# Grouped attention's product with the values: from eight f32 matmuls a group to eight fp32r matmuls on split operands

## The chip, the cores and the metric

The kernel runs on one core of one Trainium2 chip. The metric is device microseconds for one execution. The engines that matter here are TensorE (PE, with its weight loads as PEld), VectorE (DVE), ScalarE (ACT), GpSimd (POOL) and SyncE (SP), which issues the DMAs of the weights. The engines run side by side and are tied together by semaphores only.

## What is computed

A trunk of two layers over 256 tokens of width 2048: attention in two head groups, a recurrent block, cross-attention into 256 memory tokens and a gated feed-forward block per layer, all in f32. The change touches the second head group of the first layer: 16 query heads of 64, which share 2 key and value heads (8 queries each), in chunks of 64 tokens; every chunk sees itself and the one before it. Its core in the reference is:

```python
s = jnp.einsum('bcqkgd,bcjkd->bkgcqj', qc, kb).astype(jnp.float32) * (Dh ** -0.5)
s = jnp.where(valid[None, None, None, :, None, :], s, -1e30)
...
p = jax.nn.softmax(jnp.concatenate([s, sink], axis=-1), axis=-1)[..., :-1].astype(v.dtype)
o = jnp.einsum('bkgcqj,bcjkd->bcqkgd', p, vb)
```

The last line is the product with the values. Heads of one group share `vb`.

## The kernel before

**Weights.** All weights come as one stream of units (128 x 1024 values) through four slots. For each unit ACT rounds the f32 values to fp32r (`w_hi`, line 309) and DVE subtracts that from the values (`w_lo`, line 315). A product of such split operands is made of three fp32r matmuls: high by high, high by low, low by high. ACT's split of a unit waits until PE has used the unit four before it, since the slot must be free.

**Attention.** Its 32 heads go through in eight groups of four heads, `g` = 0 to 7. Groups 0 to 3 are the first head group, 4 to 7 the second. Each has these steps:
- PE: `scores(g)` into PSUM banks 0 to 2.
- DVE: `softmax(g)`: mask or bias, row maxima (line 1406 and on), which free the banks. ACT: `exps(g)`, the exponentials with row sums. DVE: `normalise(g)` (line 1431).
- PE: `turn(g)`, twelve transposes of 128x128 (line 632) into banks 3 to 5. The first 128 queries see one block of 128 keys, the last 128 two, so every head has three blocks.
- ACT copies banks 3 and 4 to `probsT` (line 1000), DVE bank 5 (line 1420).
- PE: `values(g)`, eight matmuls in f32 (line 647) into banks 4 and 5. Even heads of the group go to one bank and odd heads to the other. For groups 4 to 7 the stationary operand is `bv2`, which holds the 64 value columns twice, so that the result of a head stands in the upper and in the lower 64 partitions, of which one half is kept.
- DVE: `outputs(g)`, two copies of 64x512 to `oT` (line 1438). After the last group ACT and DVE split `oT` into `a_hi` (line 1031) and `a_lo` (line 1444) for the output projection, whose matmuls are lines 342 and 346.

**The order.** Every engine runs its own list, written out by hand. Between the attention steps PE has 32 weight units of the memory's key and value projection (lines 382 and 387), which keep it busy while the other engines work. For group `g` PE's list is: scores of `g+1`, one unit, `turn(g)`, one unit, `values(g)`, then two units (one in groups 5 and 6, none in 7). DVE's list is: softmax of `g+1`, its part of the transposed copy of `g`, splits of two units, outputs of `g`, normalising of `g+1`, splits of the units that are left. ACT's list is: the split of a unit, its part of the transposed copy of `g`, exponentials of `g+1`, the splits of the other units. In groups 1 and 5 DVE also makes the mean squares of the memory's keys (line 1297), GpSimd raises them to the power -1/2 (line 1792), and DVE scales the keys (line 1382); in group 6 PE transposes them. In group 7 DVE makes the first two low parts of `oT` before `outputs(7)`.

The first lines of `turn` and `values` hold the waits that matter: `turn(g)` waits for `normalise(g)`, for ACT's copy of group `g-1` and for `outputs(g-1)`. `values(g)` waits for both copies of group `g`.

Of the kernel before, what the change touches and what calls it, by code (L numbers as in the profile page):

```python
# [16 lines left out]
P = 128  # L17
D_MODEL, SEQ, N_MEM = 2048, 256, 256
KT = D_MODEL // P
TT = SEQ // P  # L20
# [12 lines left out]
COLS = 512  # L33
# [48 lines left out]
def trunk(nc, t):  # L82
# [3 lines left out]
    with ctx:  # L86
# [80 lines left out]
        assert O0 + 16384 + 1536 + 2048 <= FFN  # L167
        probs = at("probs", XG, [2, 3 * COLS])
        probsT = at("probsT", XG + 12288, [3 * COLS])
        bv2 = at("bv2", XG + 24576, [TT, B_KV_HEADS, 2, HEAD_DIM])  # L170
        bias_at = [at("bias0", FFN + size([4, SEQ + 2]) + size([4, SEQ]), [3 * COLS]), at("bias1", XG + 12288 + 6144, [3 * COLS])]
        mem_sq = [at("mem_sq0", FFN + 4096, [TT, XA_W]), vmem[1]]

# [49 lines left out]
        exp_done, prob_ready, bv2_ready = sem("exp_done"), sem("prob_ready"), sem("bv2_ready")  # L223
        pT_ps, pT_act, pT_dve, o_ps, o_done = sem("pT_ps"), sem("pT_act"), sem("pT_dve"), sem("o_ps"), sem("o_done")
        oT_hi, oT_lo = sem("oT_hi"), sem("oT_lo")

        proj_free = sem("proj_free")

# [297 lines left out]
        def block_done(name, b0, pos):  # L526
# [3 lines left out]
                return q if u == UNITS[name] - 1 else None  # L530
            return pos // UNITS[name] if pos % UNITS[name] == UNITS[name] - 1 else None

        def head_of(j):

            return 2 * (j % 2) + j // 2
# [3 lines left out]
        def _(pe):  # L539
# [80 lines left out]
            def turn(g):  # L620
                pb = probs[:, g % 2, :]

                pe.wait_ge(prob_ready, g + 1)
                if g:

                    pe.wait_ge(pT_act, g)
                    pe.wait_ge(o_done, g)

                for o in range(4):
                    for e, src in enumerate((8 + o, 2 * o, 2 * o + 1)):  # L630
                        n = 3 * o + e
                        last = nc.tensor.transpose(ps[:, 3 + n // 4, (n % 4) * P:(n % 4 + 1) * P], pb[:, src * P:(src + 1) * P],  # L632
                                                   ident[:, :])
                last.then_inc(pT_ps, 1)

            def values(g):

                pe.wait_ge(pT_act, g + 1)
                pe.wait_ge(pT_dve, g + 1)
                if g == 4:  # L640
                    pe.wait_ge(bv2_ready, 1)
                for j in range(4):
                    o, pair = 3 * head_of(j) * P, 2 * g + j // 2

                    for kt in range(TT):
                        val = v[:, kt, pair * P:(pair + 1) * P] if g < 4 else bv2[:, kt, (g - 4) // 2, :, :].rearrange("p e d -> p (e d)")
                        last = nc.tensor.matmul(ps[:, 4 + j % 2, (j // 2) * SEQ + kt * P:(j // 2 + 1) * SEQ], val,  # L647
                                                probsT[:, o + 2 * kt * P:o + (2 + kt) * P],
                                                start=kt == 0, stop=kt == 1, skip_group_check=True)
                last.then_inc(o_ps, 1)  # L650

            def turn_keys(l, g):
# [14 lines left out]
            for g in range(8):  # L667
                after_scores, after_turn, after_values = BETWEEN[g]
                if g < 7:
                    scores(g + 1)  # L670
                for f in after_scores:
                    mem_unit(f)
                turn(g)
                for f in after_turn:
                    mem_unit(f)
                values(g)
                for f in after_values:
                    if f == after_values[-1] and g in KEYS_TURNED:
                        turn_keys(KEYS_TURNED[g], g)
                    mem_unit(f)  # L680
# [188 lines left out]
        def _(act):  # L869
# [125 lines left out]
            def transposed(g):  # L995
# [3 lines left out]
                    act.wait_ge(o_ps, g)  # L999
                A(probsT[:, 0:2 * COLS], flat(ps[:, 3:5, :]), ACT.Copy).then_inc(pT_act, 1)  # L1000

            ch.link(act, A(lam[:, 0, :], rconst[:, :, 7], ACT.Abs))
            A(lam[:, 1, :], lam[:, 0, :], ACT.Exp, scale=-1.0).then_inc(sp_exp, 1)
# [5 lines left out]
            for g in range(8):  # L1010
                after_scores, after_turn, after_values = BETWEEN[g]
                if g in MEM_EVAC:
                    mem_evac(MEM_EVAC[g])
                for f in after_scores:
                    split_next(f)
                transposed(g)
                if g < 7:
                    exps(g + 1)
                for f in after_turn:
                    split_next(f)  # L1020
                for f in after_values:
                    if f == after_values[-1] and g in KEYS_TURNED:
                        keys_turned(KEYS_TURNED[g])
                    split_next(f)
# [242 lines left out]
        def _(dve):  # L1267
# [117 lines left out]
            def softmax(g):  # L1385
                pb, nm = probs[:, g % 2, :], neg_max[:, g % 2, :]
                dve.wait_ge(s_ps, g + 1)
                if g >= 2:

                    dve.wait_ge(pT_ps, g - 1)  # L1390
                s = HEAD_DIM ** -0.5
                if g < 4:
                    dve.wait_ge(bias_ok, g + 1)
                    last = V.scalar_tensor_tensor(pb, flat(ps[:, 0:3, :]), s, bias_at[g % 2][:, :], ALU.mult, ALU.add)
                else:
                    V.scalar_tensor_tensor(pb[:, 0:2 * COLS].rearrange("p (h n) -> p h n", h=4),
                                           flat(ps[:, 0:2, :]).rearrange("p (h n) -> p h n", h=4), s,
                                           mask[:, 0:SEQ].unsqueeze(1).to_broadcast([P, 4, SEQ]), ALU.mult, ALU.add)
                    last = V.scalar_tensor_tensor(pb[:, 2 * COLS:].rearrange("p (h n) -> p h n", h=4),
                                                  ps[:, 2, :].rearrange("p (h n) -> p h n", h=4), s,  # L1400
                                                  mask[:, SEQ:SEQ + P].unsqueeze(1).to_broadcast([P, 4, P]), ALU.mult, ALU.add)
                last.then_inc(s_used, 1)
                dve.wait_ge(s_used, g + 1)
                if g >= 2:
                    dve.wait_ge(exp_done, g - 1)
                V.tensor_reduce(nm[:, 0:4], pb[:, 0:2 * COLS].rearrange("p (h n) -> p h n", h=4), op=ALU.max, axis=X)
                ch.link(dve, V.tensor_reduce(nm[:, 4:8], pb[:, 2 * COLS:].rearrange("p (h n) -> p h n", h=4), op=ALU.max, axis=X))
                if g < 4:
                    V.tensor_scalar(nm, nm, -1.0, None, ALU.mult).then_inc(nmax_ready, 1)
                else:  # L1410
                    ch.link(dve, V.tensor_tensor(nm, nm, sinks[:, g - 4, :], ALU.max))
                    ch.link(dve, V.tensor_scalar(nm, nm, -1.0, None, ALU.mult))
                    V.tensor_tensor(sink_e[:, g % 2, :], sinks[:, g - 4, :], nm, ALU.add).then_inc(nmax_ready, 1)

            def transposed(g):
# [3 lines left out]
                    dve.wait_ge(o_ps, g)  # L1419
                V.tensor_copy(probsT[:, 2 * COLS:3 * COLS], ps[:, 5, :]).then_inc(pT_dve, 1)  # L1420

            def normalise(g):

                dve.wait_ge(exp_done, g + 1)
                sm, pb = sums[:, g % 2, :], probs[:, g % 2, :]
                if g >= 4:
                    ch.link(dve, V.tensor_tensor(sm, sm, sink_e[:, g % 2, :], ALU.add))
                ch.link(dve, V.reciprocal(rsum[:, :], sm))
                for cols, heads, keys in ((slice(0, 2 * COLS), slice(0, 4), SEQ), (slice(2 * COLS, 3 * COLS), slice(4, 8), P)):
                    x = pb[:, cols].rearrange("p (h n) -> p h n", h=4)  # L1430
                    last = V.tensor_tensor(x, x, rsum[:, heads].unsqueeze(2).to_broadcast([P, 4, keys]), ALU.mult)
                last.then_inc(prob_ready, 1)

            def outputs(g):
# [3 lines left out]
                    last = V.tensor_copy(flat(oT[part, 2 * g:2 * g + 2, :]), ps[part, 4 + e, :])  # L1438
                last.then_inc(o_done, 1)

            def low_outputs(b):

                dve.wait_ge(oT_hi, b + 1)
                V.tensor_tensor(pair_tiles(a_lo, 2 * b, 2), oT[:, 2 * b:2 * b + 2, :], pair_tiles(a_hi, 2 * b, 2).bitcast(F),  # L1444
                                ALU.subtract).then_inc(oT_lo, 1)
# [7 lines left out]
            for g in range(8):  # L1453
                after_scores, after_turn, after_values = BETWEEN[g]
                if g < 7:
                    softmax(g + 1)
                transposed(g)
                for f in after_scores:
                    split_next(f)
                if MEM_EVAC.get(g) in (0, 2):  # L1460
# [4 lines left out]
                    keys_normed(MEM_EVAC[g] // 2)  # L1465
                if g == 7:

                    dve.wait_ge(pT_act, 8)
                    dve.wait_ge(yT_done, len(NORMED) + 2)
                    for _ in range(2):  # L1470
                        V.engine_nop().then_inc(proj_free, 1)
                    for b in range(2):
                        low_outputs(b)
                outputs(g)
                if g < 7:
                    normalise(g + 1)
                for f in after_values:
# [1 line left out]
                if g == 0:  # L1479

                    dve.wait_ge(tok_free, TOK.index("bkv") + 1)
                    for e in range(2):
                        last = V.tensor_copy(bv2[:, :, :, e, :], bv[:, :, :].rearrange("p t (h d) -> p t h d", h=2))
                    last.then_inc(bv2_ready, 1)
            for b in range(2, 8):
                low_outputs(b)

# [516 lines left out]
```

## Time and profile before

| | us |
|---|---|
| median of 3 runs | 2323.28 (2323.11 to 2323.39) |
| profiled execution | 2323.38 |
| its span on the core | 2321.7 |
| PE busy in the span | 2299.5 (99%) |
| DVE busy | 1580.0 (68%) |
| ACT busy | 1243.2 (54%) |
| granted clock of PE, mean | 1.00 |

The profile shows one execution. A line of a view names the kernel line, the engine, the operation and the tiles (result <- operands) with partitions x elements. A time in brackets at the end of a row is idle time of that engine just before it, and who ended it. Matmuls overlap, so the time from one start to the next says more than the duration of one.

### The profile page before, as it was taken

To read this page: it belongs to the slowest core of one execution; us is meant where nothing else is said; L and a number is where in the kernel's file an instruction comes from. 1 tells how busy PE (TensorE), PEld (TensorE's weight loads), DVE (VectorE), ACT (ScalarE), POOL (GpSimd) and SP (SyncE) were. 2 spreads that over 40 slices of the span, in tenths; PEclk is the share of its full clock that TensorE was granted. 3 is DMA by queue.
4 is the path that set the end of the run, shared out by engine and by line. 5 is a ranking of instruction groups with operands and counts; after the bars stand their busy time and mean duration, and the time that the engine had idled before them with its cause. 6 is when DMAs were issued, how large, how long until landed. Compare 5 with 4: busy or idle time off the path is not lost.

```text
span 2321.7 us, 38274 instructions
## 1 busy us (share of the span) xinstructions
PE 2299.5 (99%) x13164; PEld 2002.4 (86%) x13164; DVE 1580.0 (68%) x1958; ACT 1243.2 (54%) x1701; POOL 205.8 (9%) x188
## 2 busy tenths in 40 slices
PE   8999999999999999999999999999999999999999
PEld 6888888988888888888888888898888888888888
DVE  7766776577777777755556778667777777774443
ACT  5655555465555555544444776555555555553332
POOL 5620001230000000000000100222000000000000
PEclk9999999999999999999999999999999999999999
DMA  7556435544555555565555555545555555556554
GB/s 269 201 195 199 132 121 178 172 154 164 198 187 184 183 189 197 190 196 189 190 190 184 180 189 178 199 134 177 176 196 191 191 181 183 197 190 199 187 187 160
DMA packets 118941, 426.93 MB, mean 184 GB/s; under 512 B 13600, under 2 KB 14496, under 8 KB 118864
## 3 DMA queue, kind: packets, MB, share of 16 engines
q1 hardware_dynamic: 117072, 418.36, 54.0%
q0 software_dynamic: 1792, 7.52, 1.0%
q8 instruction: 51, 0.84, 0.2%
q14 instruction: 26, 0.21, 0.0%
HBM read 423.73 MB, written 2.10 MB: 183 GB/s over the span
## 4 chain that ended last, share of the span: by engine, by line
PE 95%; DVE 3%; ACT 1%; issue 1%; DMA 0%; SPq 0%; ACTq 0%; DVEq 0%
PE ps L342 51%; PE ps L346 25%; PE ps L382 7%; PE ps L387 4%; PE ps L327 2%; PE ps L363 2%; DVE w_lo L315 1%; PE ps L647 1%; PE ps L834 1%; ACT w_hi L309 0%; PE ps L632 0%; DVE xg_hl L1273 0%; PE ps L717 0%; DMA xT<-in_x_t 0%; PE ps L556 0%
## 5 line engine op out<-in xcount | busy, mean ns | idle before, releaser
L315 DVE TENSOR_TENSOR w_lo<-raw,w_hi 128x1024 fp32r<-128x1024 f32 x788 | 961.6, 1241 | 497.4 <-ACT w_hi L309 493.0
L309 ACT ACTIVATE w_hi<-raw 128x1024 fp32r<-128x1024 f32 x787 | 812.3, 1056 | 558.6 <-PE ps L346 420.5
L342 PE MATMUL ps<-xg_hl,w_hi 128*128 128x512 f32 x3328 | 1047.0, 396 | 5.9 <-DVE w_lo L315 5.9
L346 PEld LDWEIGHTS ps<-xg_hl,w_lo 128*128 128x128 f32 x3328 | 625.2, 188 | 147.8
L346 PE MATMUL ps<-xg_hl,w_lo 128*128 128x256 f32 x3328 | 653.8, 278 | 0.0
L342 PE MATMUL ps<-a_hl,w_hi 128*128 128x512 f32 x1920 | 603.0, 395 | 0.6 <-DVE a_hl L1444 0.6
L342 PEld LDWEIGHTS ps<-xg_hl,w_hi 128*128 128x128 f32 x3328 | 506.9, 189 | 7.3 <-DVE w_lo L315 7.1
L346 PEld LDWEIGHTS ps<-a_hl,w_lo 128*128 128x128 f32 x1920 | 360.7, 188 | 85.3
L346 PE MATMUL ps<-a_hl,w_lo 128*128 128x256 f32 x1920 | 377.1, 278 | 0.0
L342 PEld LDWEIGHTS ps<-a_hl,w_hi 128*128 128x128 f32 x1920 | 292.2, 189 | 0.7 <-DVE w_lo L315 0.7
L1154 ACT ACTIVATE y_buf<-u_buf,fconv 128x256 f32<-128x256 f32 x176 | 96.7, 597 | 231.1 <-DVE u_buf L1619 231.1
L382 PE MATMUL ps<-w_hi,xg_hl 128*128 128x512 f32 (+1 forms) x576 | 137.9, 383 | 7.4 <-DVE xg_hl L1273 6.4
L1626 DVE SCALAR_TENSOR_TENSOR y_buf<-u_buf,fconv,y_buf 128x256 f32<-128x256 f32 x176 | 85.2, 485 | 82.4 <-ACT y_buf L1154 81.7
L382 PEld LDWEIGHTS ps<-w_hi,xg_hl 128*128 128x128 f32 x576 | 104.1, 190 | 28.1 <-issue 6.9
L1149 ACT ACTIVATE a_hl<-y_buf 128x512 f32 (+1 forms) x44 | 27.9, 633 | 103.9 <-DVE y_buf L1648 103.9
L1662 DVE TENSOR_TENSOR u_buf<-cross,ps 128x512 f32<-128x512 f32 x84 | 57.8, 688 | 34.4 <-ACT cross L1188 34.3
L1631 DVE SCALAR_TENSOR_TENSOR y_buf<-u_buf,fconv,y_buf 128x256 f32<-128x256 f32 x176 | 77.1, 480 | 0.1
L387 PE MATMUL ps<-w_lo,xg_hl 128*128 128x512 f32 (+1 forms) x288 | 73.9, 381 | 1.2 <-DVE w_lo L315 1.1
L382 PE MATMUL ps<-w_hi,a_hl 128*128 128x512 f32 x256 | 66.1, 400 | 0.9 <-ACT kmem_tok L967 0.6
L387 PEld LDWEIGHTS ps<-w_lo,xg_hl 128*128 128x128 f32 x288 | 52.1, 189 | 13.0 <-DVE w_lo L315 3.2
L1140 ACT ACTIVATE y_buf<-y_buf 128x512 f32<-128x512 f32 x44 | 27.9, 634 | 61.2 <-DVE y_buf L1631 61.1
L1273 DVE SCALAR_TENSOR_TENSOR xg_hl<-xT,gains,xg_hl 128x256 fp32r<-128x256 f32 (+1 forms) x96 | 55.2, 601 | 7.7 <-ACT xg_hl L874 7.5
(197 smaller groups left out, 1533.7 us busy)
## 6 DMA issues: line engine op xcount, KB each, us to landing
raw<-in_w_stream SPq DMA_DIRECT2D x787, 512.0 KB, 4.1
bias<-in_rel_bias POOLq DMA_DIRECT2D x4, 768.0 KB, 6.3
memT<-in_mem_t POOLq DMA_DIRECT2D x4, 512.0 KB, 6.6
gate_w<-in_gate_w POOLq DMA_DIRECT2D x4, 512.0 KB, 3.9
out_t<-xT SPq DMA_DIRECT2D x8, 256.0 KB, 4.1
xT<-in_x_t SPq DMA_DIRECT2D x2, 512.0 KB, 8.6
xT<-in_x_t SPq DMA_DIRECT2D x3, 256.0 KB, 7.7
raw<-in_w_stream SPq DMA_DIRECT2D x2, 256.0 KB, 3.2
```

Of the source, the lines that this page charges most:

```text
L309: nc.scalar.activation(w_hi[:, s, :], raw[:, s, :], ACT.Copy).then_inc(hi_done, 1)
L315: nc.vector.tensor_tensor(w_lo[:, s, :], raw[:, s, :], w_hi[:, s, :].bitcast(F), ALU.subtract).then_inc(lo_done, 1)
L327: last = nc.tensor.matmul(ps[:, bank, 0:SEQ], a[:, s, w], b[:, k0 + k, :], start=start and k == 0 and q == 0, stop=stop and k == nk - 1 an ...
L342: nc.tensor.matmul(ps[:, bank + m, :], w_hi[:, s, w], both, start=start and k == ks[0], stop=False, skip_group_check=True)
L346: last = nc.tensor.matmul(ps[:, bank + m, SEQ:2 * SEQ], w_lo[:, s, w], x[:, xk, 0, :], start=False, stop=stop and k == ks[-1], skip_group_ ...
L382: nc.tensor.matmul(ps[:, bank + tt, 0:n], a[:, k0 + k, tt * P:tt * P + P], w_hi[:, s, k * n:k * n + n], start=start and k == 0 and q == 0, ...
L387: last = nc.tensor.matmul(ps[:, bank + tt, 0:n], hi[:, k0 + k, tt * P:tt * P + P], w_lo[:, s, k * n:k * n + n], start=False, stop=stop and ...
L1154: A(y_buf[:, m, :], u_buf[:, m, 2:2 + SEQ], ACT.Identity, scale=column(fconv, w + 2, i, 32), bias=column(fconv, w + 3, i, 32)).then_inc(ta ...
L1273: V.scalar_tensor_tensor(dst, src, gain, hi.bitcast(F), ALU.mult, ALU.subtract).then_inc(count, 1)
L1626: middle.append(ch.mark(V.scalar_tensor_tensor(y_buf[:, m, :], u_buf[:, m, 1:1 + SEQ], column(fconv, 4 * (4 * half + m) + 1, i, 32), y_buf ...
L1631: ins = V.scalar_tensor_tensor(y_buf[:, m, :], u_buf[:, m, 0:SEQ], column(fconv, 4 * (4 * half + m), i, 32), y_buf[:, m, :], ALU.mult, ALU ...
L1662: V.tensor_tensor(u_buf[:, tile:tile + 2, 2:2 + SEQ], cross[:, :, :], ps[:, bank:bank + 2, 0:SEQ], ALU.add).then_inc(proj_free, 1)
```

## The change

The product of groups 4 to 7 is made of fp32r matmuls on split operands. `bv_hlh` takes the place of `bv2` and holds high, low, high of the 64 value columns. Its columns 0 to 127 (high, low) are the stationary operand for the even heads of a group, columns 64 to 191 (low, high) that for the odd ones. So one matmul gives the product with the high values in the half that belongs to the head, and the product with the low values in the other. The transposed probabilities are split too: ACT rounds them to `pT_hi`, in three copies of one bank each, and DVE subtracts to `pT_lo`, in three instructions. Two heads with the same half go through one matmul: 512 columns for the first block of keys, 256 for the second, once with `pT_hi` and once with `pT_lo`. Then ACT copies the two halves with the low product to `o_low`, across the partitions, and DVE's `outputs` becomes an addition. The product of low by low is included. Groups 0 to 3 are as before.

```diff
-        bv2 = at("bv2", XG + 24576, [TT, B_KV_HEADS, 2, HEAD_DIM])
+        pT_hi = at("pT_hi", XG + 12288, [3 * COLS], R)
+        pT_lo = at("pT_lo", XG + 12288 + 6144, [3 * COLS], R)
+        bv_hlh = at("bv_hlh", XG + 24576, [TT, B_KV_HEADS, 3, HEAD_DIM], R)
+        o_low = at("o_low", XG + 24576 + 3072, [COLS])
...
+        def turned(g):
+
+            return g + 2 * max(0, g - 4)
+
...
-                last.then_inc(pT_ps, 1)
+                        if n == 11 or (g >= 4 and n % 4 == 3):
+                            last.then_inc(pT_ps, 1)
...
+            def grouped_values(g):
+
+
+                pe.wait_ge(pT_act, turned(g + 1))
+                pe.wait_ge(pT_dve, turned(g + 1))
+                if g == 4:
+                    pe.wait_ge(bv2_ready, 1)
+                hi4, lo4 = (z[:, :].rearrange("p (o b n) -> p o b n", o=4, b=3) for z in (pT_hi, pT_lo))
+                for e in range(2):
+                    out = ps[:, 4 + e, :].rearrange("p (o n) -> p o n", o=2)
+                    for kt in range(TT):
+                        val = bv_hlh[:, kt, (g - 4) // 2, e:e + 2, :].rearrange("p e d -> p (e d)")
+                        for x, part in enumerate((hi4, lo4)):
+                            p = part[:, 2 * e:2 * e + 2, 2, :] if kt else part[:, 2 * e:2 * e + 2, 0:2, :].rearrange("p o b n -> p o (b n)")
+                            last = nc.tensor.matmul(out[:, :, kt * P:SEQ], val, p, start=kt == 0 and x == 0, stop=kt == 1 and x == 1,
+                                                    skip_group_check=True)
                 last.then_inc(o_ps, 1)
...
+            def transposed_hi(g):
+                act.wait_ge(o_ps, g)
+                for x in range(3):
+                    act.wait_ge(pT_ps, turned(g) + x + 1)
+                    A(pT_hi[:, x * COLS:(x + 1) * COLS], ps[:, 3 + x, :], ACT.Copy).then_inc(pT_act, 1)
+
+            def low_halves(g):
+
+                act.wait_ge(o_ps, g + 1)
+                if g > 4:
+                    act.wait_ge(o_done, g)
+                A(o_low[0:64, :], ps[64:P, 4, :], ACT.Copy)
+                A(o_low[64:P, :], ps[0:64, 5, :], ACT.Copy).then_inc(o_low_ready, 1)
+
...
                 for f in after_turn:
                     split_next(f)
+                if g >= 4:
+                    low_halves(g)
...
+            def transposed_lo(g):
+                dve.wait_ge(o_ps, g)
+                for x in range(3):
+                    dve.wait_ge(pT_act, turned(g) + x + 1)
+                    cols = slice(x * COLS, (x + 1) * COLS)
+                    V.tensor_tensor(pT_lo[:, cols], ps[:, 3 + x, :], pT_hi[:, cols].bitcast(F), ALU.subtract).then_inc(pT_dve, 1)
+
...
+            def grouped_outputs(g):
+                dve.wait_ge(o_low_ready, g - 3)
+                for e in range(2):
+                    part = slice(64 * e, 64 * e + 64)
+                    last = V.tensor_tensor(flat(oT[part, 2 * g:2 * g + 2, :]), ps[part, 4 + e, :], o_low[part, :], ALU.add)
                 last.then_inc(o_done, 1)
...
-                    for e in range(2):
-                        last = V.tensor_copy(bv2[:, :, :, e, :], bv[:, :, :].rearrange("p t (h d) -> p t h d", h=2))
-                    last.then_inc(bv2_ready, 1)
+                    whole = bv[:, :, :].rearrange("p t (h d) -> p t h d", h=2)
+                    for x in (0, 2):
+                        V.tensor_copy(bv_hlh[:, :, :, x, :], whole).then_inc(bv_hi, 1)
+                    dve.wait_ge(bv_hi, 2)
+                    V.tensor_tensor(bv_hlh[:, :, :, 1, :], whole, bv_hlh[:, :, :, 0, :].bitcast(F), ALU.subtract).then_inc(bv2_ready, 1)
```

What stands in a row on PE, at the product of group 4, before. The names are result <- operands:

```order
L387 MATMUL ps<-w_lo,a_hl 128x512 x3
L647 MATMUL ps<-probsT,bv_101 128x256 [waits bv2_ready,pT_dve,pT_act]
L647 MATMUL ps<-probsT,bv_101 128x128
L647 MATMUL ps<-probsT,bv_101 128x256
L647 MATMUL ps<-probsT,bv_101 128x128
L647 MATMUL ps<-probsT,bv_101 128x256
L647 MATMUL ps<-probsT,bv_101 128x128
L647 MATMUL ps<-probsT,bv_101 128x256
L647 MATMUL ps<-probsT,bv_101 128x128
L382 MATMUL ps<-w_hi,a_hl 128x512 [waits hi_done]
```

And the same place after:

```order
L391 MATMUL ps<-w_lo,a_hl 128x512 x3
L674 MATMUL ps<-pT_hi,bv_hlh 128x512 [waits bv2_ready,pT_dve,pT_act]
L674 MATMUL ps<-pT_lo,bv_hlh 128x512
L674 MATMUL ps<-pT_hi,bv_hlh 128x2x128
L674 MATMUL ps<-pT_lo,bv_hlh 128x2x128
L674 MATMUL ps<-pT_hi,bv_hlh 128x512
L674 MATMUL ps<-pT_lo,bv_hlh 128x512
L674 MATMUL ps<-pT_hi,bv_hlh 128x2x128
L674 MATMUL ps<-pT_lo,bv_hlh 128x2x128
L386 MATMUL ps<-w_hi,a_hl 128x512 [waits hi_done]
```

The product stays at its place between the same weight units, with as many instructions, each of them wider.

DVE in group 6, from the end of the softmax of group 7, before:

```order
L1413 TENSOR_TENSOR sink_e<-sinks,neg_max 128x8 [waits dve_self]
L1420 COPY probsT<-ps 128x512 [waits o_ps,pT_ps]
L315 TENSOR_TENSOR w_lo<-raw,w_hi 128x1024 [waits hi_done] x2
L1438 COPY oT<-ps 64x512 [waits o_ps]
L1438 COPY oT<-ps 64x512
```

DVE there after:

```order
L1461 TENSOR_TENSOR sink_e<-sinks,neg_max 128x8 [waits dve_self]
L1475 TENSOR_TENSOR pT_lo<-ps,pT_hi 128x512 [waits pT_act,o_ps]
L1475 TENSOR_TENSOR pT_lo<-ps,pT_hi 128x512 [waits pT_act] x2
L319 TENSOR_TENSOR w_lo<-raw,w_hi 128x1024 [waits hi_done] x2
L1500 TENSOR_TENSOR oT<-ps,o_low 64x512 [waits o_low_ready]
L1500 TENSOR_TENSOR oT<-ps,o_low 64x512
```

One copy became three subtractions that wait for ACT's parts, and the outputs wait for ACT's `o_low` in place of PE.

ACT in group 7, from its part of the transposed copy to the first high parts of `oT`, before:

```order
L1000 ACTIVATE probsT<-ps 128x1024 [waits o_ps,pT_ps]
L309 ACTIVATE w_hi<-raw 128x1024 [waits pe_unit,raw_full3]
L1031 ACTIVATE a_hl<-oT 128x2x256 [waits o_done,pe_unit]
L1031 ACTIVATE a_hl<-oT 128x2x256 [waits o_done]
L967 ACTIVATE vmem_60<-ps,r_tok 128x512 [waits rtok_ready,pe_unit]
```

ACT there after:

```order
L1035 ACTIVATE pT_hi<-ps 128x512 [waits pT_ps,o_ps]
L1035 ACTIVATE pT_hi<-ps 128x512 [waits pT_ps] x2
L313 ACTIVATE w_hi<-raw 128x1024 [waits pe_unit,raw_full3]
L1042 ACTIVATE o_low<-ps 64x512 [waits o_done,o_ps]
L1043 ACTIVATE o_low<-ps 64x512
L1079 ACTIVATE a_hl<-oT 128x2x256 [waits o_done,pe_unit]
L1079 ACTIVATE a_hl<-oT 128x2x256 [waits o_done]
L996 ACTIVATE vmem_60<-ps,r_tok 128x512 [waits rtok_ready,pe_unit]
```

The two copies to `o_low`, which wait for the product of group 7 (`o_ps`), stand ahead of the first high part of `oT`.

## Rows read from the trace of the kernel before

**Rows 1.** The page: busy time of each engine, and the chain that ended last.

```profile
PE 2299.5 (99%) x13164; PEld 2002.4 (86%) x13164; DVE 1580.0 (68%) x1958; ACT 1243.2 (54%) x1701; POOL 205.8 (9%) x188
...
PE 95%; DVE 3%; ACT 1%; issue 1%; DMA 0%; SPq 0%; ACTq 0%; DVEq 0%
```

**Rows 2.** Waits of PE, 290 to 348 us: us in total, times, longest.

```profile
PE ps L647 <- DVE probsT L1420: 0.8, 1, 0.8
PE ps L342 <- DVE a_hl L1444: 0.6, 1, 0.6
PE ps L382 <- ACT kmem_tok L967: 0.3, 1, 0.3
```

**Rows 3.** Groups by line and shape: busy us, mean ns of one, idle before.

```profile
L1188 ACT ACTIVATE cross<-ps 128x512 f32<-128x512 f32 x104 | 60.0, 577 | 0.0
...
L1503 DVE TENSOR_TENSOR xT<-xT,ps 128x512 f32<-128x512 f32 x16 | 11.0, 687 | 14.0 <-PE ps L346 14.0
...
L647 PE MATMUL ps<-probsT,bv 128*128 128x256 f32 x32 | 9.6, 382 | 0.8 <-DVE probsT L1420 0.8
...
L647 PE MATMUL ps<-probsT,bv 128*128 128x128 f32 x32 | 6.2, 274 | 0.0
```

**Rows 4.** Timeline of PE, then DVE, in group 4: start, duration.

```profile
297.81 2.78 PE L647 MATMUL ps<-probsT,bv 128*128 128x256 f32 x16
300.35 2.07 PE L382 MATMUL ps<-w_hi,a_hl 128*128 128x512 f32 x8
...
295.55 0.68 DVE L1420 COPY probsT<-ps 128x512 f32<-128x512 f32 x1
```

**Rows 5.** Timeline of PE in the output projection.

```profile
347.97 0.63 PE L342 MATMUL ps<-a_hl,w_hi 128*128 128x512 f32 x2
348.43 0.40 PE L346 MATMUL ps<-a_hl,w_lo 128*128 128x256 f32 x2
348.67 0.62 PE L342 MATMUL ps<-a_hl,w_hi 128*128 128x512 f32 x2
```

**Rows 6.** Timeline of DVE in group 1.

```profile
247.92 1.23 DVE L315 TENSOR_TENSOR w_lo<-raw,w_hi 128x1024 fp32r<-128x1024 f32 x1 [2.36 <-ACT w_hi L309]
```

**Rows 7.** Timelines of PE, DVE and POOL in group 5.

```profile
315.37 2.78 PE L647 MATMUL ps<-probsT,bv 128*128 128x256 f32 x16
...
312.80 0.69 DVE L1420 COPY probsT<-ps 128x512 f32<-128x512 f32 x1
...
319.71 1.22 DVE L1382 TENSOR_TENSOR kmem_tok<-kmem_tok,rq 128x1024 f32<-128x1024 f32 x1
320.85 1.39 DVE L1438 COPY oT<-ps 64x512 f32<-64x512 f32 x2
...
316.04 1.66 POOL L1792 TENSOR_TENSOR rq<-ss,neg_half 128x8 f32<-128x8 f32 x1 [63.69 <-DVE ss L1299]
```

**Rows 8.** Timelines of PE and DVE, groups 6 and 7.

```profile
330.72 2.86 PE L647 MATMUL ps<-probsT,bv 128*128 128x256 f32 x16 [0.76 <-DVE probsT L1420]
...
339.76 1.50 PE L632 MATMUL ps<-ident,probs 128*128 128x128 f32 x12
...
329.89 0.69 DVE L1420 COPY probsT<-ps 128x512 f32<-128x512 f32 x1
...
336.00 1.38 DVE L1438 COPY oT<-ps 64x512 f32<-64x512 f32 x2
```

**Rows 9.** Timelines of PE, ACT and DVE, end of group 7.

```profile
343.85 2.78 PE L647 MATMUL ps<-probsT,bv 128*128 128x256 f32 x16
347.19 0.70 PE L342 MATMUL ps<-a_hl,w_hi 128*128 128x512 f32 x2 [0.56 <-DVE a_hl L1444]
...
344.11 1.06 ACT L309 ACTIVATE w_hi<-raw 128x1024 fp32r<-128x1024 f32 x1 [1.78 <-PE ps L387]
345.07 1.14 ACT L1031 ACTIVATE a_hl<-oT 128x512 fp32r<-128x512 f32 x2
...
346.36 1.30 DVE L1444 TENSOR_TENSOR a_hl<-oT,a_hl 128x512 fp32r<-128x512 f32 x2
```

More of the change, by code:

```diff
@@ L225, in trunk @@
         oT_hi, oT_lo = sem("oT_hi"), sem("oT_lo")
+        bv_hi, o_low_ready = sem("bv_hi"), sem("o_low_ready")
         proj_free = sem("proj_free")
@@ L624, in turn @@
                 if g:
-                    pe.wait_ge(pT_act, g)
+                    pe.wait_ge(pT_act, turned(g))
+                    pe.wait_ge(pT_dve, turned(g))
                     pe.wait_ge(o_done, g)
@@ L633, in turn @@
                                                    ident[:, :])
-                last.then_inc(pT_ps, 1)
+                        if n == 11 or (g >= 4 and n % 4 == 3):
+                            last.then_inc(pT_ps, 1)
             def values(g):
[L638 to L641, printed above, removed]
+                pe.wait_ge(pT_act, turned(g + 1))
+                pe.wait_ge(pT_dve, turned(g + 1))
                 for j in range(4):
@@ L645, in values @@
                     for kt in range(TT):
-                        val = v[:, kt, pair * P:(pair + 1) * P] if g < 4 else bv2[:, kt, (g - 4) // 2, :, :].rearrange("p e d -> p (e d)")
+                        val = v[:, kt, pair * P:(pair + 1) * P]
                         last = nc.tensor.matmul(ps[:, 4 + j % 2, (j // 2) * SEQ + kt * P:(j // 2 + 1) * SEQ], val,
@@ L649, in values @@
                                                 start=kt == 0, stop=kt == 1, skip_group_check=True)
+                last.then_inc(o_ps, 1)
+            def grouped_values(g):
+                pe.wait_ge(pT_act, turned(g + 1))
+                pe.wait_ge(pT_dve, turned(g + 1))
+                if g == 4:
[9 more added lines that the diff above has]
+                                                    skip_group_check=True)
                 last.then_inc(o_ps, 1)
@@ L675, in _ @@
                     mem_unit(f)
-                values(g)
+                if g < 4:
+                    values(g)
+                else:
+                    grouped_values(g)
                 for f in after_values:
@@ L1015, in _ @@
                     split_next(f)
-                transposed(g)
+                if g < 4:
+                    transposed(g)
+                else:
+                    transposed_hi(g)
                 if g < 7:
@@ L1388, in softmax @@
                 if g >= 2:
-                    dve.wait_ge(pT_ps, g - 1)
+                    dve.wait_ge(pT_ps, turned(g - 1))
                 s = HEAD_DIM ** -0.5
@@ L1439, in outputs @@
                 last.then_inc(o_done, 1)
+            def grouped_outputs(g):
[3 more added lines that the diff above has]
+                    last = V.tensor_tensor(flat(oT[part, 2 * g:2 * g + 2, :]), ps[part, 4 + e, :], o_low[part, :], ALU.add)
+                last.then_inc(o_done, 1)
             def low_outputs(b):
@@ L1456, in _ @@
                     softmax(g + 1)
-                transposed(g)
+                if g < 4:
+                    transposed(g)
+                else:
+                    transposed_lo(g)
                 for f in after_scores:
@@ L1466, in _ @@
                 if g == 7:
-                    dve.wait_ge(pT_act, 8)
+                    dve.wait_ge(pT_act, turned(8))
                     dve.wait_ge(yT_done, len(NORMED) + 2)
@@ L1473, in _ @@
                         low_outputs(b)
-                outputs(g)
+                if g < 4:
+                    outputs(g)
+                else:
+                    grouped_outputs(g)
                 if g < 7:
```

## The prediction

> **What bounds the kernel now.** The page comes first. TensorE (PE) is busy 99% of the span, and the chain that ended last lies on it for 95% [rows 1]. So a microsecond taken from PE's stream is a microsecond of the kernel, as long as nothing else is late where it is taken. The next question is where PE is not the bound. I looked at the stretch that the change touches, groups 4 to 7 of the attention, 290 to 348 us. The waits of PE there are three and add up to 1.7 us [rows 2]: one on VectorE (DVE) for the transposed probabilities, one on DVE for the first tile of the next section, and a small one on ScalarE (ACT). The first two touch what the change makes longer. So the stretch must be walked through group by group, with the time of each engine; PE's busy share alone would mislead.
>
> **The product itself.** One group's eight f32 matmuls (each in two passes, so 16 records; the four groups have 32 of each width [rows 3]) stream 1,536 columns, and take 2.54 us from the first start to the start of the next weight unit, 297.81 to 300.35 [rows 4]. The new product has eight fp32r matmuls as well, four of 512 and four of 256 columns: 3,072 columns. Their price is not in this trace for two-part moving data, but the fp32r matmuls of the output projection have the same widths: two of 512 and two of 256 columns per step, and a step is 0.70 us, 347.97 to 348.67 [rows 5]. Twice that is 1.40 us. The bounds are 1.40 and, if the piecewise moving data took away all gain, the old 2.54; I take 1.40, since the runs of 128 or 256 neighbouring values differ little from the 512 of those rows. **Saved: 1.14 us a group, 4.6 us in all.** That is also the most that the change can give, and it is just under 0.2% of 2323.
>
> The Trainium skill, page "TensorE: Matmul & The Clock Gate", section "Back-to-back issue gap", gives about 131 ns for a matmul of 512 columns in a stream of weight loads and matmuls, and 81 ns for 128. By that, with some 100 ns for 256 columns, the product would be an estimated 0.9 us and the saving 1.6 us a group. The same rule would make the step of the output projection 0.46 us, where the trace has 0.70 [rows 5], so it is not taken here; it would change the result below by about -0.5 us.
>
> **What is added elsewhere.** (a) ACT: the copy of the transposed probabilities becomes three of 128x512 instead of one of 128x1024. Such a copy out of PSUM is 0.58 us [rows 3], so three are some 1.6 with overlap. They may begin after four of twelve transposes. (b) DVE: the one copy of 0.69 us becomes three subtractions of a PSUM and an SBUF operand, 0.69 us each by the residual addition of that shape [rows 3], 2.05 together (bounds 1.9 to 2.1). **DVE's part comes 1.4 us later than now, each time.** It stands after the softmax of the next group on DVE's queue, as before. (c) ACT: two copies of 64x512 that bring the low product to the other half, about 1.1 us, and DVE's output additions now wait for them; the additions themselves cost what the copies did. (d) DVE once, after group 0: a subtraction more, and one wait on itself, about +0.5 us; DVE sits idle for 2.36 us soon after, before the weight unit at 247.92 [rows 6], and PE does not wait there, so it costs nothing. No DMA and nothing on SyncE or GpSimd is added.
>
> **Group by group**, as PE's shift against the trace (minus is earlier).
> Group 4: the product starts at 297.81. DVE's old copy starts at 295.55 [rows 4]; the first high part is there by about then, so the three subtractions end near 297.65. No wait, by 0.1 to 0.2 us. After the product PE is at -1.1. ACT's exponentials begin some 0.3 us later, and with the low halves behind them the outputs of group 4 come about 0.3 later on DVE. I take this as absorbed before the softmax of group 6; if not, add 0.3.
> Group 5: the old copy starts at 312.80 [rows 7], held up by the softmax ahead of it, so the subtractions end at 314.9. PE, 1.1 early, is at the product at 314.3 instead of 315.37: it now waits 0.6 and starts at -0.4, and leaves at **-1.55**. On DVE the sum of squares of the memory keys comes 1.4 later, GpSimd's power of 1.66 us [rows 7] ends at 319.1 instead of 317.7, and the scaling of the keys starts there, still 0.55 ahead of the old 319.71, which waited for a weight unit. The weight unit is early because the exponentials are. So the outputs at 320.85 and everything behind them on DVE move by -0.55.
> Group 6: this is where DVE is the bound. The old copy starts at 329.89 and PE waits 0.76 for it [rows 8]. Now the start is 329.35, and three subtractions end at 331.4. PE, which comes at 328.3, waits 3.2 us and starts at 331.5 instead of 330.72. Here the whole gain so far is given back: **+0.75** at the start, -0.4 after the product. ACT's low halves then lie beside DVE's weight unit, so the outputs (now 336.00) are at -0.5, and the transposes of group 7, which waited for DVE at 339.76 [rows 8], are at -0.5.
> Group 7: no softmax is ahead, so the subtractions end under the weight unit. The product starts at 343.35 instead of 343.85, and ends at 344.75.
> The next section: its first matmul at 347.19 waits for the low part of the first tile on DVE, 346.36 to about 347.05 [rows 9]. That chain now runs from the end of the last weight unit (about 343.9) over ACT's split at 344.11 and DVE's. The change puts the low halves of group 7 on ACT ahead of the first high part (345.07), and they wait for the end of the product: 344.75, +0.25 for the signal, +1.1 for two copies, +0.55 for the high part, +0.7 for the low one, +0.05: 347.4. So the new chain is 4.0 us long from the end of that unit where the old was 3.3. **PE starts there at +0.2**, although it was done 1.6 us earlier. The later tiles follow: DVE's output additions and the third pair's low part end near 350.0, and PE, 2.8 us into the section, asks for it at 350.2. From here on the rest is PE's stream, shifted by +0.2.
>
> In gaps: 4 x -1.14 saved, +0.65 waiting in group 5, +2.3 in group 6, +1.8 before the next section, together +0.2. The profiled execution took 2323.38 with a span of 2321.7, and its time is 0.1 from the median 2323.28. **Forecast: 2323.5 us**, that is, no change.
>
> **Rivals.**
> 1. The gain stays. If DVE and ACT kept up in groups 5 and 6, PE would reach the end of the last weight unit at 3 x -1.14 = -3.4, and the new chain of 4.0 instead of 3.3 us would give +0.75 back: 2320.6. For it: three of four products start without DVE's delay today [rows 2]. Against it: group 6 already waits, and its delay grows by construction. 0.10, spread from 2320.5 to 2322.3.
> 2. The change doesn't do what it says: the new product takes as long as the old (2.54), since the moving data come in pieces. Then group 6 starts at +1.3 and keeps that, and the last chain adds 1.14 + 0.75: +3.2, 2326.5. 0.12, with the cases in between, in which ACT's or DVE's new instructions are dearer than their rows.
> 3. Slower: fp32r falls back to the f32 rate on these operands. A column then costs 2.54/1,536 us [rows 4], 3,072 of them 5.1 us, 2.5 more than now in each of four groups, with the last chain's 0.75 and group 6's 1.3: about +12, 2335. It decides for slower from some 3.4 us a group on. Against it: the fp32r steps of the projections run at 0.70 us for 1,536 columns [rows 5]. 0.04.
> 4. The forecast, with the terms' bounds (0.3 in group 4, 0.2 on each set of subtractions, some 0.1 on each signal): 2322.3 to 2324.8. 0.72. Something else that I don't see has 0.02.
>
> The likeliest case and what lies near it give the range: **2321.9 to 2325.7**. A measurement of this kernel tells a change from none at about 0.2%, 4.6 us. Faster by more would need more than the whole saving: 0.02. Slower by more is rival 3 and a rest: 0.05. Within: 0.93.
>
> **What the profile after would show.** The product: eight fp32r matmuls in 1.4 us from the first start to the next unit (2.5: rival 2, 5: rival 3). PE's waits on DVE's low part: none in group 4, 0.6 us in group 5, about 3 in group 6; if group 6 waits under 1.5, rival 1 is near. Before the output projection a gap of 2.6 us, ended by DVE's first low part, with ACT's two 64x512 copies just ahead of the first high part. Everything after 350 us at a constant shift of a few tenths. The forecast is wrong if that shift is not constant, or if the power on GpSimd, which now sets the outputs of group 5, comes later than 319.1.

## The result, and the profile after

The changed kernel takes 2326.35 us (median of 22 runs, 2323.43 to 2327.66), the kernel before 2323.09 in the same sessions (22 runs, 2322.26 to 2324.3). The ratio is 1.0012, with a 95% interval of 1.0007 to 1.0018: slower by 0.12%, about 3 us. That is less than the 0.2% that the forecast called a change, and 0.65 us above the upper end of its range of 2321.9 to 2325.7. The profiled execution took 2326.14 us with a span of 2324.3, against 2323.38 and 2321.7.

The page and the waits of PE between 290 and 350 us, which answer to [rows 1, 2]. The waits read: us in total, times, longest:

```profile
PE 2297.8 (99%) x13132; PEld 2000.1 (86%) x13132; DVE 1584.8 (68%) x1967; ACT 1247.9 (54%) x1717; POOL 206.8 (9%) x188
```

```profile
PE ps L674 <- DVE pT_lo L1475: 3.3, 2, 2.9
PE ps L346 <- DVE a_hl L1506: 2.8, 1, 2.8
PE ps L386 <- ACT kmem_tok L996: 0.3, 1, 0.3
```

PE is busy 1.7 us less in the whole span, and waits 4.7 us more in these rows. The waits on DVE are where the forecast had them: before the products of groups 5 and 6, and before the output projection.

The timeline of PE at the products of groups 4 to 7 and at the output projection, to be read against [rows 4, 7 to 9]; columns are start, duration, and in brackets the idle time before and who ended it:

```profile
297.62 0.39 PE L674 MATMUL ps<-pT_hi,bv_hlh 128*128 128x512 f32 x1
...
299.01 2.00 PE L386 MATMUL ps<-w_hi,a_hl 128*128 128x512 f32 x8
...
314.51 0.47 PE L674 MATMUL ps<-pT_hi,bv_hlh 128*128 128x512 f32 x1 [0.41 <-DVE pT_lo L1475]
...
315.97 2.00 PE L386 MATMUL ps<-w_hi,a_hl 128*128 128x512 f32 x8
...
330.82 0.62 PE L674 MATMUL ps<-pT_hi,bv_hlh 128*128 128x512 f32 x1 [2.86 <-DVE pT_lo L1475]
331.24 0.63 PE L674 MATMUL ps<-pT_lo,bv_hlh 128*128 128x512 f32 x1
...
333.38 1.54 PE L685 MATMUL ps<-ident,kmem_tok 128*128 128x128 f32 x8
334.67 2.09 PE L386 MATMUL ps<-w_hi,a_hl 128*128 128x512 f32 x8
...
340.25 1.47 PE L641 MATMUL ps<-ident,probs 128*128 128x128 f32 x12
...
344.33 0.39 PE L674 MATMUL ps<-pT_hi,bv_hlh 128*128 128x512 f32 x1
...
348.64 1.19 PE L346 MATMUL ps<-a_hl,w_hi 128*128 128x512 f32 x2 [2.76 <-DVE a_hl L1506]
...
350.06 1.05 PE L346 MATMUL ps<-a_hl,w_hi 128*128 128x512 f32 x2
...
351.34 0.69 PE L346 MATMUL ps<-a_hl,w_hi 128*128 128x512 f32 x2
```

In groups 4 and 5 the product takes 1.39 and 1.46 us. In group 6 the same eight matmuls take 2.56, from 330.82 to 333.38, and those of 512 columns follow each other by 0.42 us instead of 0.23. The first two steps of the output projection take 1.42 and 1.28 us, where a step takes 0.70 [rows 5]. Why, the view of stretches tells. Its columns are the stretch, its length, PE's busy time (matmuls), the granted clock, the DMA share and GB/s:

```profile
320.00:330.80 10.80, 7.96 (x45) 1.00 0.27 93
330.80:334.60 3.80, 3.77 (x15) 0.55 0.43 134
334.60:345.70 11.10, 11.10 (x59) 1.00 0.31 97
345.70:348.60 2.90, 0.18 (x2) 0.91 0.67 212
348.60:351.30 2.70, 2.66 (x8) 0.50 0.49 161
351.30:356.00 4.70, 4.70 (x28) 0.98 0.00 0
```

After each of the two waits of 2.8 us the granted clock is at its lower level, 0.50 or 1.2 GHz. The mean of 0.55 over the first 3.80 us says that some 3.4 us of them run at that level. At the second place it is at least the 2.7 us up to the third step, and the 0.91 of the row before says that the clock fell some 0.5 us ahead of the first matmul. From there on almost nothing more is lost: the third step begins at 351.34, 2.67 us later than in [rows 5], and the span is 2.6 us longer.

The kernel before has one wait of 0.8 and one of 0.6 us there and keeps the clock at 1.00. Its same stretches:

```profile
330.80:334.60 3.80, 3.80 (x26) 1.00 0.42 136
345.70:348.60 2.90, 2.34 (x15) 1.00 0.43 138
```

### The profile page after: what moved, and what is told of

Its sections match the earlier page's. It is cut to its first block, busy times and chain, and to the rows that moved or that the text cites. A ratio compares the mean times of both kernels' runs of the same rounds, so it can differ in the third digit from the quotient of the medians.

```text
span 2324.3 us, 38245 instructions
## 1 busy us (share of the span) xinstructions
PE 2297.8 (99%) x13132; PEld 2000.1 (86%) x13132; DVE 1584.8 (68%) x1967; ACT 1247.9 (54%) x1717; POOL 206.8 (9%) x188
## 4 chain that ended last, share of the span: by engine, by line
PE 95%; DVE 3%; ACT 1%; issue 1%; DMA 0%; SPq 0%; ACTq 0%; DVEq 0%
PE ps L346 51%; PE ps L350 25%; PE ps L386 7%; PE ps L391 4%; PE ps L331 2%; PE ps L367 2%; DVE w_lo L319 1%; PE ps L863 1%; ACT w_hi L313 0%; PE ps L655 0%; DVE xg_hl L1321 0%; PE ps L641 0%; PE ps L746 0%; DMA xT<-in_x_t 0%; PE ps L564 0%
```

## The experiments

Two theories stood at the start. A: the loss against the forecast is the clock, which falls because of the new waits. B: the matmuls after the waits are slow for a reason of their own, the operands in pieces or the other engines at work beside them.

**fill_both.** PE gets work that nobody needs in the two waits.

```diff
+            def filler(n):
+                pe.wait_ge(s_used, 8)
+                for _ in range(n):
+                    nc.tensor.matmul(ps[:, 2, 0:P], ident[:, :], ident[:, :], start=True, stop=True)
...
                 else:
+                    if g == 6:
+                        filler(12)
                     grouped_values(g)
...
                         turn_keys(KEYS_TURNED[g], g)
                     mem_unit(f)
+            filler(12)
```

> The changed kernel with PE kept busy in its two long waits: twelve f32 matmuls of identity by identity (128 columns each, into a PSUM bank that is free) before the product of group 6, and twelve before the output projection. They add nothing to the path, since PE only waits there. Theory A (the loss against the prediction is the clock, granted at half after each of the two waits of 2.8 us): the granted clock stays at 1.0, the product of group 6 takes 1.40 us again instead of 2.56, and the time falls by the lost part, some 2.5 to 3 us, to 2323.3 to 2323.9. Theory B (the matmuls after a long wait are slow for a reason of their own, such as the three-part operands or DVE and ACT working beside them): they stay at 2.56 us, and the time stays at 2326.3 or rises.

Measured: 2323.62 us (11 runs, 2322.82 to 2324.83), ratio to the kernel before 1.0001 (0.9992 to 1.0010). The stretches of this kernel, columns as above:

```profile
330.80:334.60 3.80, 3.63 (x23) 1.00 0.38 112
334.60:345.70 11.10, 11.10 (x63) 1.00 0.37 114
345.70:348.60 2.90, 2.82 (x21) 1.00 0.88 305
348.60:351.30 2.70, 2.70 (x17) 1.00 0.06 23
```

And its timeline of PE at the two places:

```profile
331.08 0.47 PE L674 MATMUL ps<-pT_hi,bv_hlh 128*128 128x512 f32 x1 [0.17 <-DVE pT_lo L1483]
...
332.56 1.03 PE L685 MATMUL ps<-ident,kmem_tok 128*128 128x128 f32 x8
...
347.40 0.70 PE L346 MATMUL ps<-a_hl,w_hi 128*128 128x512 f32 x2
```

The clock stays at 1.00, the product of group 6 takes 1.48 us, and the output projection begins at 347.40. The same operands and the same neighbours, but no loss: B falls. Work that is thrown away makes the changed kernel 2.7 us faster, 2323.62 against 2326.35; the kernel before took 2323.17 beside the one and 2323.09 beside the other.

**fill_g6.** Only the first filling.

```diff
                 else:
+                    if g == 6:
+                        filler(12)
                     grouped_values(g)
```

> Only the first of the two fillings, before the product of group 6. Theory A: the clock stays up there, and falls still before the output projection; about half of the loss comes back, 2324.6 to 2325.2, and the profile has one stretch at 0.5 instead of two. Theory B: no change, 2326.3.

Measured: 2324.80 us (10 runs, 2323.14 to 2325.33), in the expected place: half of the loss is back. The profiled execution was not the one that was expected. It took 2323.41 us, and shows no stretch at half clock although the wait before the output projection is there:

```profile
PE ps L346 <- DVE a_hl L1513: 2.8, 1, 2.8
```

So a wait of 2.8 us does not lower the clock every time. That fits the runs: two of the ten have a mean granted clock of 1.000, and took 2323.14 and 2323.41; the eight at 0.999 took 2324.34 to 2325.33. None of the eight was profiled. Here and below, the mean clock of a run that was not profiled is a sign and no proof: 3.4 us at half clock lower a mean over 2324 us by an estimated 0.0007, and 0.999 does not say where the clock was low. Single runs of the kernel before have it too, and so has the fastest run of early_norm_fill.

**high_first.** ACT makes the first two high parts of the attention output ahead of the low halves of group 7.

```diff
-                if g >= 4:
+                if 4 <= g < 7:
                     low_halves(g)
...
                 if b == 2:
+                    low_halves(7)
                     mem_evac(3)
```

> The changed kernel with ACT's two low halves of group 7 behind the first two high parts of the attention output instead of ahead of them. The first low part on DVE then waits for the split of the last weight unit (345.69 + 1.23), as before the change. The theory that the low halves there set the end of the chain: PE begins the output projection about 1.0 us earlier, waits 1.8 to 1.9 us instead of 2.8, and if the clock then stays up, another 1.3 us comes back there: 2323.9 to 2324.6. If only the wait is shortened and the clock falls all the same: 2325.3. If the low halves are hidden: 2326.3.

Measured: 2323.96 us (11 runs, 2322.5 to 2325.82). In the profiled execution (2325.48 us) the wait is shorter by 1.0 us, and the clock falls after it nonetheless:

```profile
347.72 0.70 PE L346 MATMUL ps<-a_hl,w_hi 128*128 128x512 f32 x2 [1.80 <-DVE a_hl L1507]
```

```profile
347.70:351.50 3.80, 3.78 (x13) 0.58 0.58 189
347.72:348.30 0.58, 0.58 (x3) 1.00 0.75 304
```

The order on ACT did set the end of that chain: the projection begins 0.9 us earlier than in the changed kernel. The mean of 0.58 over 3.80 us says that some 3.2 us of them ran at the lower level, and the first two matmuls, 0.70 us from 347.72 on, are as fast as in [rows 9]: the clock fell after PE had begun. This execution lost time in group 6 as well: its product starts at 330.91 after a wait of 2.85 us, and the next weight unit 3.85 us later, as in the changed kernel. The clock falls after 1.8 us too, in some runs: three lie at 2325.4 to 2325.8 and seven at 2323.4 to 2324.2, all with a mean clock below 1.000; the eleventh, at 1.000, took 2322.5. That the seven had one fall and the three two is what their times suggest; only one, of the three, was profiled. The median is where the expectation had it for a clock that stays up behind the shorter wait.

**before_delay4.** The kernel before, with a longer wait in group 6 and nothing else.

```diff
+                for _ in range(4 if g == 6 else 0):
+                    ch.link(dve, V.tensor_copy(probsT[:, 2 * COLS:3 * COLS], ps[:, 5, :]))
                 V.tensor_copy(probsT[:, 2 * COLS:3 * COLS], ps[:, 5, :]).then_inc(pT_dve, 1)
```

> The kernel before, with four more copies of 128x512 on DVE ahead of its part of the transposed probabilities in group 6, each linked to the one before it: some 2.8 to 3.0 us. No fp32r product, no low halves. PE's wait of 0.76 us in group 6 becomes 3.6 to 3.8. Theory A: the clock falls here too, and the f32 product and what follows it run at half rate for about 3.8 us, which costs 1.9 more: 2323.1 + 2.9 + 1.9 = 2327.9. Theory B (it belongs to the new product): only the delay, 2326.0.

Measured: 2327.73 us (10 runs, 2326.12 to 2329.84), ratio 1.0020 (1.0011 to 1.0030). The old f32 product in group 6, and the granted clock there:

```profile
332.43 5.46 PE L647 MATMUL ps<-probsT,bv 128*128 128x256 f32 x16 [3.64 <-DVE probsT L1422]
```

```profile
332.40:336.20 3.80, 3.77 (x12) 0.50 0.41 127
336.20:345.00 8.80, 8.80 (x47) 0.91 0.24 66
```

5.46 us where [rows 8] have 2.86. The second mean, 0.91 over 8.80 us, adds some 1.6 us to the 3.8 at the lower level: 5.4 us of matmuls at half rate, where 3.8 were expected. And the clock was there before the first of them, while PE still waited:

```profile
331.00:332.40 1.40, 0.00 (x0) 0.50 0.00 0
```

PE waited 2.9 us longer than in the kernel before, and the product took 2.6 longer, 5.5 in all. The time is 4.6 us longer by the medians and 4.3 by the profiled executions. The rest is the start of the kernel: this execution is 1.2 us ahead at the weight unit before the wait (328.90 in the kernel before, then 327.73 here), and was so at 22 us already.

```profile
328.90 1.07 PE L387 MATMUL ps<-w_lo,a_hl 128*128 128x512 f32 x4
```

```profile
327.73 1.07 PE L387 MATMUL ps<-w_lo,a_hl 128*128 128x512 f32 x4
```

The effect needs nothing of the new product; a wait is enough.

**before_delay2.** The same with two copies (`range(2 if g == 6 else 0)`).

> The kernel before, with two more linked copies on DVE in group 6 instead of four: some 1.5 us. PE's wait becomes 2.2 to 2.3 us. If the clock only falls after waits of nearly 3 us: 2324.6. If it falls after this one too, in part of the runs: 2324.6 in some and 2326 to 2326.5 in the others.

Measured: 2326.2 us (10 runs, 2324.5 to 2326.7). The wait is 2.2 us, and in the profiled execution (2326.54 us) the clock falls:

```profile
332.38 4.41 PE L647 MATMUL ps<-probsT,bv 128*128 128x256 f32 x16 [2.19 <-DVE probsT L1422]
```

```profile
332.30:335.00 2.70, 2.62 (x8) 0.50 0.20 41
```

The runs part as the expectation had it for a clock that falls in part of them: three with a mean clock of 1.000 took 2324.5 to 2325.3, the seven below it 2325.9 to 2326.7.

**early_norm.** Where does the gain of the product go once the clock is left out? To the order of DVE's list, or to its load? This kernel is high_first with other lists; these lines show them in part, without the splits of group 5 that move.

```diff
 # ACT
+                if 4 <= g < 7:
+                    low_halves(g)
                 for f in after_turn:
                     split_next(f)
-                if 4 <= g < 7:
-                    low_halves(g)
...
 # DVE
-                else:
+                elif g == 6:
+                    keys_normed(1)
+                    transposed_lo(g)
+                    split_next(25)
+                    split_next(26)
+                else:
                     transposed_lo(g)
...
+                if 4 <= g < 7:
+                    normalise(g + 1)
+                    grouped_outputs(g)
-                for f in after_turn:
-                    split_next(f)
+                if g != 5:
+                    for f in after_turn:
+                        split_next(f)
```

> The changed product in another order on ACT and DVE. ACT: the low halves of groups 4 to 6 come ahead of the splits of the weight units, and the first two high parts ahead of the low halves of group 7. DVE: in groups 4 to 6 the normalising and the outputs come ahead of the splits, and in group 5 two splits and the scaling of the memory's keys move behind the softmax of group 7. Theory (the gain of the product was spent in the order of DVE's list, not in its load): PE waits at most 0.5 us for the product of group 6, the transposes of group 7 start near 336, and the output projection starts some 4 us earlier than in the kernel before: 2319.1 to 2319.6 with the clock up, and 1.3 more where it falls in the wait of 1.8 us before the output projection, 2320.4. If DVE's load is the bound: the wait moves to the transposes of group 7, and the time stays at 2323 or above.

Measured: 2319.63 us (11 runs, 2319.1 to 2321.1), ratio to the kernel before 0.9987 (0.9978 to 0.9996). PE's waits from 288 to 352 us, and its timeline at the transposes of groups 6 and 7 and at the projection:

```profile
PE ps L346 <- DVE a_hl L1507: 1.8, 1, 1.8
PE ps L674 <- DVE pT_lo L1476: 0.4, 1, 0.4
PE ps L386 <- ACT kmem_tok L996: 0.3, 1, 0.3
```

```profile
328.11 0.47 PE L674 MATMUL ps<-pT_hi,bv_hlh 128*128 128x512 f32 x1 [0.37 <-DVE pT_lo L1476]
...
335.94 1.47 PE L641 MATMUL ps<-ident,probs 128*128 128x128 f32 x12
...
343.37 0.70 PE L346 MATMUL ps<-a_hl,w_hi 128*128 128x512 f32 x2 [1.79 <-DVE a_hl L1507]
```

The wait in group 6 is 0.4 us instead of 2.9, and the output projection begins at 343.37 instead of 347.19 [rows 9]. DVE has the same work, in another order. So the load was not the bound.

**early_norm_fill.** With `filler(8)` before the output projection.

> The kernel of early_norm with eight f32 matmuls of identity by identity before the output projection, 1.7 us, within the wait. Clock theory: no stretch at half clock around the attention, 2319.1 to 2319.6, with little spread. If the fillings delay the projection: 2320 or more.

Measured: 2319.30 us (11 runs, 2318.81 to 2320.24), ratio 0.9984 (0.9975 to 0.9993). This is the fastest kernel of the study, 3.8 us under the kernel before and 7 under the changed one. Against early_norm the difference is 0.3 us, and the two intervals overlap; what it takes away is the upper runs. The profiled execution keeps the clock up through the whole stretch:

```profile
326.00:345.00 19.00, 18.62 (x107) 1.00 0.60 191
```

In early_norm, with its wait of 1.8 us, the mean clock suggests few falls: three of eleven runs have it below 1.000 (2320.58 to 2321.1).

**before_order.** How much of this is the order alone? The kernel before, with the same DVE list (shown in part, too).

```diff
+                if g == 6:
+                    keys_normed(1)
                 transposed(g)
+                if g == 6:
+                    split_next(25)
+                    split_next(26)
...
+                if 4 <= g < 7:
+                    normalise(g + 1)
+                    outputs(g)
```

> The kernel before (f32 product, plain copies) with DVE's list in the order of early_norm; ACT's list has no low halves and stays. PE's waits for DVE in group 6 (0.76 us, [rows 8]) and at the transposes of group 7 (0.2) should go, nothing else: 2322.1 to 2322.3. Then of the 3.5 us by which early_norm is faster than the kernel before, 1.0 is the order and 2.5 the product. If the order alone gave all of it, 2319.6. If it gave nothing, 2323.1, and the product has all.

Measured: 2322.19 us (11 runs, 2321.57 to 2322.87), ratio 0.9995 (0.9986 to 1.0005), an interval that holds 1. PE's waits from 290 to 350 us have lost the one in group 6:

```profile
PE ps L342 <- DVE a_hl L1444: 0.6, 1, 0.6
PE ps L382 <- ACT kmem_tok L967: 0.3, 1, 0.3
```

The medians put the order at 0.9 us and the product, once the order lets it through, at 2.6. That 2.6 is less than the 4.6 us that four products save, since early_norm waits 1.8 us before the output projection and 0.4 in group 6, where this kernel waits 0.6 and nothing; it also holds the other order of ACT's list. The interval of this run alone would also allow nothing for the order.

## Why the prediction was wrong

The forecast was 2323.5 us, the time 2326.35. It lies near the 2326.5 of rival 2, but not for its reason.

**The step that failed** is the pricing of PE's waits in groups 6 and 7. "Waits 3.2 us and starts at 331.5" and "PE starts there at +0.2" counted a wait as the time in it, and everything behind it at the full rate: the product at 1.40 us in group 6, and "from here on the rest is PE's stream". The clock after a wait was left out, though the forecast had both waits at their full length. The costs, from the profiled execution: from the start of the product of group 6 to the next weight unit 3.85 us (330.82 to 334.67), against 1.40 for the product and 0.79 for the transposes of the keys at full clock, which are these rows of the kernel before: **1.65 us**.

```profile
333.42 1.04 PE L659 MATMUL ps<-ident,kmem_tok 128*128 128x128 f32 x8
334.21 2.09 PE L382 MATMUL ps<-w_hi,a_hl 128*128 128x512 f32 x8
```

In the output projection, from its first matmul to the third step, 2.70 us (348.64 to 351.34), against 1.48 in [rows 5, 9] (347.19 to 348.67): **1.2 us**. Together 2.9 us, and the median is 2.85 above the forecast. That they agree so closely is in part luck: without the 1.65 us this trace would have begun the projection at an estimated 346.99, 0.4 before the forecast's 347.4. With PE kept busy in both waits, the time is 2323.62.

The other steps, one by one:

- *The product, 1.40 us.* Right: 1.39 and 1.46 where the clock was up. Rival 2 (2.54) and rival 3 (5.1) were wrong; two heads in pieces of 128 or 256 values stream as one piece of 512 does. The Trainium skill, page "TensorE: Matmul & The Clock Gate", section "Back-to-back issue gap", gives about 131 ns for a matmul of 512 columns in a stream of weight loads and matmuls. This trace does not agree: it has 0.23 us from start to start, as the forecast judged by [rows 5].
- *ACT's copies.* Right: three take 1.55 us, the two low halves 1.2, forecast 1.6 and 1.1.
- *DVE's subtractions, 2.05 us.* Slightly too dear: three take 1.88 (312.48 to 314.36).

```profile
312.48 1.88 DVE L1475 TENSOR_TENSOR pT_lo<-ps,pT_hi 128x512 fp32r<-128x512 f32 x3
...
328.80 1.88 DVE L1475 TENSOR_TENSOR pT_lo<-ps,pT_hi 128x512 fp32r<-128x512 f32 x3
```

- *Group 5, a wait of 0.6 us; group 6, the start at 331.5.* 0.4 us, and 330.82. DVE reached the subtractions of group 6 at 328.80 instead of 329.35, since the subtractions before it and GpSimd's power (done at 318.57, which is 316.91 + 1.66, not 319.1) were earlier. This trace as a whole runs 0.2 us ahead of the one before at this point (297.62 against 297.81), so 0.35 us are left of the 0.55.
- *The chain before the output projection, 4.0 us from the end of the last weight unit.* Nearly right, 0.25 us too short: 344.33 + 1.40 for the product, then ACT's low halves at 345.92, its high part at 347.14, DVE's low part at 347.80 and PE at 348.64, which is 4.3 us from 344.33. The forecast has 347.4 - 343.35 = 4.05.

```profile
345.92 0.59 ACT L1042 ACTIVATE o_low<-ps 64x512 f32<-64x512 f32 x1 [0.27 <-PE ps L674]
346.52 0.59 ACT L1043 ACTIVATE o_low<-ps 64x512 f32<-64x512 f32 x1
347.14 1.15 ACT L1079 ACTIVATE a_hl<-oT 128x512 fp32r<-128x512 f32 x2
```

- *The one-off work on DVE after group 0.* Right: 0.43 us for the subtraction, and PE gets no new wait there.
- *No change without the clock.* Right as far as the runs tell: two of the 22 have a mean granted clock of 1.000. They took 2323.43 and 2323.58 us, and the forecast was 2323.5. Neither was profiled.

Rival 1, the gain that stays, had the right idea and the wrong kernel: early_norm reaches 2319.6, below the 2320.6 that it gave, by another order of the same work.

The forecast held that a measurement of this kernel tells a change from none at about 0.2%. That was too coarse: the change costs 0.12%, and 22 runs a side show it.

## What to carry to other kernels

A wait of the matmul engine costs more than its length where the granted clock falls after it: in the profiled executions six of eight waits of 1.8 to 3.6 us in this stretch were followed by matmuls at half rate, some 3 us of them, and 5.4 after the longest. So price a new wait as its length plus half of the stretch that runs slow behind it, look at the granted clock of short stretches, not at its mean (0.999 here), and say that the time will spread. And before an engine's load is called the bound, try the order of its list: what the waiting engine needs next should stand ahead of work that is needed much later.

## What the runs showed of the hardware that was not expected

The fall of the clock is not the same in every run. In profiles, it came after waits of 2.8 us in the changed kernel and not in fill_g6, and after 1.8 us in high_first and not in early_norm. By the mean clock of the runs, it was absent in two of 22 runs of the changed kernel, in three of ten with a wait of 2.2 us, and in most runs of early_norm. Nor does it come at a fixed place: 1.4 us before PE worked again in before_delay4, and 0.6 us after it had begun again in high_first, where the stretch from 347.72 to 348.30 is still at 1.00. The kernel before, with waits of 0.8 and 0.6 us in this stretch, spreads over 2.0 us in 22 runs, the changed kernel over 4.2. What decides in a single run was not tested. A part of the spread is not from these waits: the profiled executions of the kernels differ by 1.4 us at 23 us already (an early product with the low weights starts between 22.17 in before_delay4 and 23.57 in early_norm).

The cheapest cure that was found is odd: 24 f32 matmuls of identity by identity, whose result is never read, made the changed kernel faster by 2.7 us.
